# A product that nobody reads, after the gate products of four tokens

## The reference, cut to what matters

```
eidx = take_along_axis(cand_idx, pos)          # the chosen experts
g = softmax(top_s, axis=-1)                    # their gates
pre = einsum('cd,chkd->chk', hc, u[ec])        # h . u of the chosen experts
coef = gc * gelu(pre)
out = einsum('chk,chkd->cd', coef, v[ec])
```

## Time and profile before

| | |
|---|---|
| median of 3 runs | 1450.76 us (1448.74 to 1456.02) |
| profiled execution | 1450.47 us |
| its span, from the first to the last instruction | 1448.7 us |
| mean granted TensorE clock | 0.988 |
| TensorE busy | 1401.2 us (97%) |
| VectorE busy | 1097.8 us (76%) |
| ScalarE busy | 836.1 us (58%) |
| GpSimd busy | 360.9 us (25%) |

### The profile page before, as it was taken

One profiled execution on the slowest core, in us unless ns is written; L12 is line 12 of the kernel. 1 busy time (PEld: TensorE's weight loads), 2 busy tenths in 40 slices (PEclk: granted clock), 3 DMA queues, 4 the chain that ended last, 5 costly groups with the idle time before them and its releaser, 6 DMA issues.

```text
span 1448.7 us, 25878 instructions
## 1 busy us (share of the span) xinstructions
PE 1401.2 (97%) x10406; PEld 1301.1 (90%) x10406; DVE 1097.8 (76%) x1903; ACT 836.1 (58%) x1447; POOL 360.9 (25%) x227
## 2 busy tenths in 40 slices
PE   7999999899998999999999999999999999899997
PEld 5998899899998999999988888887889899799997
DVE  7788887567889888999756666677667667797762
ACT  4554774444454677777645445465546666776651
POOL 3216101234445100000032222344322221433200
PEclk9999999899999999999999999999999999999999
DMA  9757775455664544444557666665666536285630
GB/s 386 269 190 268 247 240 176 161 159 179 190 184 146 174 148 147 147 146 146 154 179 221 192 193 196 212 196 181 194 200 245 186 107 199 75 260 176 193 114 30
DMA packets 73721, 268.24 MB, mean 185 GB/s; under 512 B 8401, under 2 KB 9730, under 8 KB 72834
## 3 DMA queue, kind: packets, MB, share of 16 engines
q1 hardware_dynamic: 71280, 256.41, 56.1%
q10 hardware_dynamic: 1426, 7.56, 1.5%
q0 software_dynamic: 896, 2.62, 0.5%
HBM read 262.88 MB, written 3.67 MB: 184 GB/s over the span
## 4 chain that ended last, share of the span: by engine, by line
PE 81%; DVE 12%; ACT 4%; issue 1%; DMA 1%; POOL 1%; DVEq 0%; ACTq 0%; POOLq 0%
PE bank L611 80%; DVE split L1825 3%; DVE ada_acc L1860 2%; ACT split L1295 1%; DVE PR L2275 1%; DMA ringb<-in_w_ada 1%; DVE PR L2272 1%; POOL H L2644 0%; PE bank L784 0%; POOL split L2617 0%; DVE H L2366 0%; DVE PR L2280 0%; DMA vecs<-in_vecs 0%; DVE PA L2076 0%; DVE MH L1927 0%
## 5 line engine op out<-in xcount | busy, mean ns | idle before, releaser
L611 PE MATMUL bank<-H,split 128*128 128x256 f32 x5928 | 732.8, 282 | 15.9 <-DVE split L1825 7.7
L611 PEld LDWEIGHTS bank<-H,split 128*128 128x128 f32 x5928 | 710.2, 189 | 23.5 <-DVE split L1825 9.9
L1295 ACT CAST split<-ringb 128x1024 fp32r<-128x1024 f32 x350 | 365.9, 1047 | 284.5 <-PE bank L611 270.7
L2617 POOL TENSOR_TENSOR split<-ringb,split 128x1024 fp32r<-128x1024 f32 x91 | 229.0, 2517 | 665.7 <-ACT split L1295 665.7
L611 PE MATMUL bank<-split,H 128*128 128x512 f32 (+1 forms) x1728 | 391.1, 388 | 3.3 <-DVE H L2366 1.8
L1825 DVE TENSOR_TENSOR split<-ringb,split 128x1024 fp32r<-128x1024 f32 x259 | 330.9, 1280 | 77.5 <-ACT split L1295 77.4
L611 PEld LDWEIGHTS bank<-split,H 128*128 128x128 f32 x1728 | 321.3, 188 | 71.2 <-POOL split L2617 2.5
L2366 DVE TENSOR_TENSOR H<-PR,H 128x256 fp32r<-128x256 f32 x128 | 137.1, 1074 | 105.5 <-ACT H L1634 105.4
L1825 DVE TENSOR_TENSOR split<-far,split 128x1024 fp32r<-128x1024 f32 x77 | 99.7, 1303 | 33.5 <-ACT split L1295 33.4
L1295 ACT CAST split<-far 128x1024 fp32r<-128x1024 f32 x89 | 92.7, 1047 | 55.1 <-PE bank L611 43.9
L1610 ACT ACTIVATE PR<-bank 128x512 f32<-128x512 f32 (+31 forms) x59 | 28.7, 486 | 76.3 <-PE bank L611 76.3
(11 more groups left out here) (298 smaller groups left out, 1264.0 us busy)
## 6 DMA issues: line engine op xcount, KB each, us to landing
ringb<-in_u SPq DMA_DIRECT2D x128, 512.0 KB, 3.7
ringb<-in_v SPq DMA_DIRECT2D x128, 512.0 KB, 4.4
ringb<-in_w_ada SPq DMA_DIRECT2D x28, 512.0 KB, 5.3
far<-in_w_up SPq DMA_DIRECT2D x26, 512.0 KB, 4.2
far<-in_w_ada SPq DMA_DIRECT2D x20, 512.0 KB, 5.3
ringb<-in_w_up SPq DMA_DIRECT2D x17, 512.0 KB, 4.8
ringb<-in_w_pq SPq DMA_DIRECT2D x16, 512.0 KB, 3.8
far<-in_w_dn SPq DMA_DIRECT2D x14, 512.0 KB, 4.2
```

The lines of the kernel that those rows point to most:

```text
L611: return TE.matmul(o, l, r, start=start, stop=stop, skip_group_check=True)
L1295: S.copy(buf(m)[0], slots[P.slot[m]]).then_inc(hi_done, 1)
L2617: G.tensor_tensor(lo, slots[P.slot[m]], hi.bitcast(F32), ALU.subtract).then_inc(lo_g, 1)
```

## The change

After the 12 products of each group, `spread_gates(g)` claims bank 3 and issues, by g % 4: nothing for 0; a bfloat16 product of 128 x 128 by 128 x 128 for 1; a product of `H` with itself (128 x 128 by 128 x 256, the rounded float type) for 2; `ident` times a part of `cst`, which is itself `ident`, in plain float32 (128 x 128 by 128 x 128) for 3. Nobody reads bank 3 afterwards until `v` overwrites it. The increment of `t_mm` moves to the added product where there is one. Each kind occurs 16 times, 48 added products in all.

```
                     for z in range(3):
                         last = mm(o[:, i * 128:(i + 1) * 128], t_row[g % 3][:, a, :, b], t_gate[g % 3][:, z, a, :, b], z == 0, z == 2)
+
+                idle = claim(3)
+                if g % 4 == 1:
+                    last = mm(idle[:, 0:128], t_row[g % 3][:, 0, :, 0], t_gate[g % 3][:, 0, 0, :, 0], True, True)
+                elif g % 4 == 2:
+                    last = mm(idle[:, 0:T], H[:, 0, 0, 0:128], H[:, 0, 0, :], True, True)
+                elif g % 4 == 3:
+                    last = mm(idle[:, 0:128], ident, cst[:, 0:128], True, True)
                 last.then_inc(t_mm, 1)
                 freed[g % 3] = (t_out, g + 1)
```

## The result

The changed kernel takes 1458.44 us (median of 20 runs, 1452.38 to 1462.91), the kernel before, run beside it, 1452.52 us (20 runs, 1447.93 to 1456.71). The ratio is 1.0042, with a 95% interval of 1.003 to 1.0055. That is 6.1 us slower, within the 0.5% line, and the interval reaches a little past it. The forecast was 1457.2 us, or 0.44% over before. The measured time stands 1.2 us above it, but the kernel before stands 1.8 us above the 1450.76 us of three runs on which the forecast was built, so the two are best compared by the ratio, 0.42% against 0.44%.

A forecast was written before the change was run, and what follows sets the result against it. TensorE alone was taken to bound the stretch of `spread_gates`, with no idle time to hide products. Unrounded terms 0.86, 1.95 and 3.55 us sum to 6.4 us, on the 1450.76 us median giving 1457.2 us; range 1453 to 1463 us.

The forecast's parts named there:

- bfloat16: Behind groups with g % 4 == 1: 16 products at 54 ns, 0.9 us, bounded above by 1.2 us.
- `H` with `H`: Behind groups with g % 4 == 2: 16 products, each like a unit's 25th, 122 ns, 2.0 us; bounds 1.7 and 2.0 us.
- plain float32: Behind groups with g % 4 == 3: 16 products of two records each, 0.222 us, 3.6 us; bounds 3.4 and 4.3 us.
- The moved increment: `t_mm` comes 0.05 to 0.22 us later in three groups of four; priced at nothing, as VectorE already waits for TensorE.
- the claim of bank 3: `claim(3)` in `spread_gates` refers to a copy several units old, so it was said to cost nothing.
- the slack of VectorE: In the late window VectorE has 3.8 us to spare in 19.5 steps, 0.20 us a step, covering the later increment.
- The drain: Rival: each lone added product costs its full duration, 16.8 us in all, 1467.6 us, slower by 1.2%; chance 0.11.
- The rule of an isolated product: Skill page's rule that an isolated product cannot hide its drain and costs full latency; said to bear on the first rival.
- The second rival: Part of the delay is taken back behind the stretch, giving 1452.1 to 1455.4 us; chance 0.11.
- Its first half: A slower TensorE shortens its 1.8 us wait between `u` and `v`, leaving 4.6 us, 1455.4 us.
- Its second half, the clock: Work in two later windows finds a higher granted clock, recovering up to 5.1 us and leaving 1.3 us, 1452.1 us.
- the 81 ns: Skill page's sustained spacing of weight load and 128-column product; would make the bfloat16 term 1.3 us instead of 0.9.

The follow-up runs named there:

- e6: Kernel before with 29 plain float32 products behind the last unit of `u`, none behind the gates; timed ratio 1.004 (1.002 to 1.0061) in 10 runs.
- e8: Kernel before with 7 plain float32 products behind the last unit of `u`, none behind the gates; one run, 2.7 us over the kernel before.
- e1: Kernel before with one bfloat16 product behind all 64 groups; one run, -0.3 us against it; 1.40 us longer over 63 steps.
- e2: Kernel before with one product of `H` with `H` behind all 64 groups; one run, 9.8 us over it; 7.28 us longer over 63 steps.
- e3: Kernel before with one plain float32 product behind all 64 groups; one run, 11.5 us over it; 14.00 us longer over 63 steps.
- e5: Kernel before with one bfloat16 product in the middle of each of 64 units; one run, 8.2 us over it; 7.98 us longer over 63 steps.
- e7: Changed kernel with the `t_mm` increment left on the last gate product for `H` with `H` and plain float32; 231.39 us over 63 steps, 0.10 us less.
- e4: Changed kernel with each of the 48 added products issued four times in a row; timed ratio to the kernel before 1.0147 (1.0099 to 1.0195), 5 runs.
- e12: Kernel before with a plain float32 product ahead of the gate products in all 64 groups; one run, 6.9 us over; 12.75 us longer over 63 steps.
- e10: Kernel before with a bfloat16 product of 32 moving columns behind each group; one run, 1.0 us over it; 1.40 us longer over 63 steps.

## Why the prediction was right

**The place.** The step that decided it was that TensorE has no idle time in the stretch, so that every added product is paid. It held: no idle time after the change, and the same products cost 4.4 instead of 6.4 us, or nothing, where there is a hole (e6, e8).

**The prices.** By the medians of the steps:

| term | predicted | in the changed kernel | in all 64 groups |
|---|---|---|---|
| bfloat16 | 54 ns, 0.86 us | 55 ns, 0.9 us | 56 ns (e1) |
| `H` with `H` | 122 ns, 1.95 us | 115 ns, 1.8 us | 115 ns (e2) |
| plain float32 | 222 ns, 3.55 us | 221 ns, 3.5 us | 223 ns (e3) |
| units behind the bfloat16 ones | 0 | five quick ones, -0.5 us | 21 quick ones, -2.1 us (e1) |
| sum | 6.4 us | 5.8 us | |

The price of `H` with `H` was a little high. I had divided the time of a whole unit by 24 and written that the changes of type were in it. They are, some 70 ns by e5, and the added product doesn't pay that. The spacing inside a unit, 118 ns, would have been nearer. The other missed term is the quick pace of five units. Both lower the sum, to 5.8 us. That is under the 6.0 us to which the prediction's own lower bounds add up, as none of them allowed for a unit that becomes quicker. The chain's 5.86 us has 0.10 us more, which the unit in front of group 0 took. The time of the runs, 5.9 us between the medians and 6.1 us by the ratio, can't tell 5.8 from 6.4.

**What was priced at nothing.** The moved increment (e7), the claim of bank 3 and the slack of VectorE held. VectorE waits more by what TensorE is slower, in the change (6.0 us), e3 (14.4 us) and e4 (24.8 us). Its cover was never gone.

**The rivals.** The drain is refuted by e2, e3 and e4, and e5 shows the nearest thing to it: a lone bfloat16 product amid a unit costs 126 ns, still far from its latency of 230 ns there. The rule of an isolated product in the Trainium skill's page "TensorE: Matmul & The Clock Gate" ("Step-by-step: what each phase is for") thus does not bear on single products in a full stream. Nor did the 81 ns of its section "Back-to-back issue gap" show for bfloat16, where e1 measured 56 to 57 ns.

The second rival, that a part is taken back behind the stretch, splits in two. Its first half, a shorter wait before `v`, did not happen: the wait is 1.8 us as before. Its second half, the clock, is not excluded by 709.8 against 709.9 us. The dip of the granted clock that the kernel before has at 1145 us is absent in the changed kernel, which has one at 1270 us instead (windows before, then after, columns as in the earlier trace rows):

```profile
1144.00:1150.00 6.00, 6.00 (x38) 5.70 (x38) 2.94 (x8) 4.26 (x10) 0.00 (x0) 0.72 0.26 85
1268.00:1275.00 7.00, 7.00 (x62) 7.00 (x61) 7.00 (x12) 5.05 (x9) 2.36 (x2) 1.00 0.98 355
...
1144.00:1150.00 6.00, 5.01 (x42) 4.69 (x42) 3.75 (x11) 5.94 (x15) 0.00 (x0) 1.00 0.56 178
1268.00:1275.00 7.00, 6.04 (x38) 6.04 (x39) 5.60 (x7) 5.05 (x8) 3.25 (x2) 0.76 0.71 237
```

Counted from the first load of `v`, the changed kernel is 1.6 us ahead of the kernel before at 1151 us and 0.1 us ahead at 1276 us. So about a quarter of the delay was taken back and lost again, and no run shows that the change did either. From the first load of `v` to the end, where no kernel of this document has a changed instruction, the traces range from 701.5 us (e12) to 714.2 us (e5). The forecast took this part as fixed. That it came out equal in the two profiled executions was luck.

## What to carry to other kernels

Where TensorE has no idle time in a stretch, an added product costs about the distance between the starts of its like, not its duration and not its share of busy time; take that distance from inside a run of equals, and look at changes of type as terms of their own. Where TensorE waits for other engines, the same product is free up to the length of the wait. And when the expected effect is as large as the scatter of the runs, compare one stretch of the trace rather than spans: here the spans differed by 4.0 us and the stretch by 5.9. A part of the kernel that nobody changed is not thereby equal in two executions.

## What the runs showed of the hardware that was not expected

- Units of equal shape run at one of two paces, 113 or 118 ns from load to load, which holds for the whole unit and in e12 for 912 loads on end. An added product of 57 ns shifts which pace the units take, and the quick unit behind one gave back 103 ns (e1), yet no kernel gained by it over the 63 steps. The same products, in a part that nobody changed, ran at either pace in the traces of different kernels. What chooses is open.
- The granted clock fell to its lower level (1.2 GHz) for a few us at other places in the two executions. The first 46 products behind the same wait of 2.3 us took 5.68 us in the kernel before (from 1266.51 us on) and 7.21 us in the changed one (from 1268.96 us on), where the clock had fallen at 1270 us.
- A bfloat16 product with 128 columns of weights takes 57 ns with 32 moving columns as with 128 (e10 and e1 both have steps of 3643 ns).
- A change from the rounded float type to bfloat16 and back costs some 70 ns (e5, with no control of another kind). Plain float32 between the unit and the gates is 22 ns cheaper than behind the gates (e12, e3).
